# A two-layer trunk with a 32-expert mixture on one Trainium2 core: first quad gathered by single row blocks, slots compared with ranks in PSUM, layer one's means ahead of copies, four fillers ahead of mixer two

## What is computed

```python
def hierarchical_moe(x, wg, bg, we, be, w_gate, w_up, w_down):
    g_prob = softmax(xt @ wg + bg); g_top_p, g_idx = top_k(g_prob, 1)      # 1 of 4 groups
    e_top_l, e_idx = top_k(e_logits_of_that_group, 2)                      # 2 of its 8 experts
    gates = softmax(e_top_l) * g_top_p
    ...                                    # tokens are sorted by expert
    hb = silu(xb @ w_gate[e]) * (xb @ w_up[e])
    return hb @ w_down[e]                  # and summed with its gate into each token
```

## Time and profile before

| | |
|---|---|
| median of three runs | 1272.65 us (1272.19 to 1274.26) |
| the profiled execution, time | 1272.65 us |
| the profiled execution, span | 1270.9 us |
| TensorE matmuls busy | 1048.5 us, 83% of the span |
| VectorE busy | 477.2 us, 38% |
| ScalarE busy | 234.7 us, 18% |
| mean granted clock of TensorE | 0.903 of full speed |
| read from memory | 459.38 MB, 362 GB/s over the span |

### The profile page before, as it was taken

One profiled execution on the slowest core, in us unless ns is written; L12 is line 12 of the kernel. 1 busy time (PEld: TensorE's weight loads), 2 busy tenths in 40 slices (PEclk: granted clock), 3 DMA queues, 4 the chain that ended last, 5 costly groups with the idle time before them and its releaser, 6 DMA issues.

```text
span 1270.9 us, 22379 instructions
## 1 busy us (share of the span) xinstructions
PE 1048.5 (83%) x9528; PEld 712.1 (56%) x9528; DVE 477.2 (38%) x1227; ACT 234.7 (18%) x526; POOL 4.9 (0%) x27
## 2 busy tenths in 40 slices
PE   9999998966777575799999999998977676758685
PEld 7888755634433342448888888865544343424243
DVE  2342543342223222236665556464344222222232
ACT  2221121111111111113433334121111111111111
POOL 1000000000000000000000000000000000000000
PEclk9999998878788887899999999999898778878799
DMA  9888699999999999995666664999999999999996
GB/s 343 235 336 330 234 422 429 425 429 429 429 429 428 429 429 429 426 392 186 207 216 226 223 215 149 348 344 418 428 428 428 430 428 429 429 428 429 429 426 278
DMA packets 96049, 461.49 MB, mean 363 GB/s; under 512 B 17260, under 2 KB 60520, under 8 KB 70632
## 3 DMA queue, kind: packets, MB, share of 16 engines
q1 hardware_dynamic: 95616, 460.34, 90.1%
q10 hardware_dynamic: 360, 0.15, 0.0%
HBM read 459.38 MB, written 1.08 MB: 362 GB/s over the span
## 4 chain that ended last, share of the span: by engine, by line
PE 55%; DMA 40%; DVE 1%; issue 1%; SPq 1%; ACT 1%; POOL 0%; POOLq 0%; DVEq 0%; ACTq 0%
DMA front<-in_expert_w_up 33%; PE pa L1767 10%; PE pa L1487 10%; PE pb L1487 8%; DMA arena<-in_expert_w_down 5%; PE wa L1767 5%; PE acc L1518 4%; PE wb L1792 3%; PE acc L1625 2%; PE pb L1735 2%; PE acc L1802 1%; PE pb L1551 1%; PE pb L1726 1%; SPq L356 1%; PE pb L1836 1%
## 5 line engine op out<-in xcount | busy, mean ns | idle before, releaser
L1767 PE MATMUL pa<-front,arena 128*32 128x256 f32 x1792 | 137.0, 473 | 90.7 <-DMA front<-in_expert_w_up 90.7
L1767 PEld LDWEIGHTS pa<-front,arena 128*32 128x32 f32 x1792 | 66.7, 135 | 163.4 <-DMA front<-in_expert_w_up 103.2
L1245 DVE TENSOR_SCALAR lower<-lower 128x128 f32<-128x128 f32 x64 | 14.4, 225 | 382.6 <-ACT lower L583 382.6
L1767 PE MATMUL wa<-front,arena 128*32 128x256 f32 x1248 | 93.5, 463 | 64.5 <-DMA front<-in_expert_w_up 60.8
L1767 PEld LDWEIGHTS wa<-front,arena 128*32 128x32 f32 x1248 | 45.6, 132 | 112.8 <-DMA front<-in_expert_w_up 69.6
L583 ACT ACTIVATE arena<-wb 32x256 f32<-32x256 f32 (+2 forms) x236 | 88.9, 377 | 105.6 <-PE wb L1792 96.8
L1792 PE MATMUL wb<-w_dn,conv_raw 128*32 128x256 f32 x1472 | 87.8, 379 | 2.5 <-DMA w_dn<-in_expert_w_down 2.5
L1735 PE MATMUL pb<-arena,hs 128*128 128x128 f32 x448 | 67.6, 313 | 26.0 <-DVE arena L1161 11.3
L1487 PE MATMUL pa<-hnT,w_x 128*128 128x256 f32 x384 | 85.1, 380 | 0.0
L1735 PEld LDWEIGHTS pb<-arena,hs 128*128 128x128 f32 x448 | 61.7, 220 | 40.4 <-DVE arena L1177 18.6
L1487 PEld LDWEIGHTS pa<-hnT,w_x 128*128 128x128 f32 x384 | 72.5, 190 | 10.0 <-issue 0.3
(11 more groups left out here) (340 smaller groups left out, 1219.8 us busy)
## 6 DMA issues: line engine op xcount, KB each, us to landing
w_dn<-in_expert_w_down SPq DMA_DIRECT2D x46, 2048.0 KB, 26.0
front<-in_expert_w_gate SPq DMA_DIRECT2D x42, 2048.0 KB, 19.0
front<-in_expert_w_up SPq DMA_DIRECT2D x42, 2048.0 KB, 23.4
w_x<-in_expert_w_gate SPq DMA_DIRECT2D x15, 2048.0 KB, 30.3
w_x<-in_expert_w_up SPq DMA_DIRECT2D x15, 2048.0 KB, 34.6
arena<-in_expert_w_down SPq DMA_DIRECT2D x14, 2048.0 KB, 26.5
w_x<-in_odd_in_proj SPq DMA_DIRECT2D x16, 1024.0 KB, 5.4
front<-in_expert_w_up SPq DMA_DIRECT2D x8, 1024.0 KB, 9.3
```

What stands on the lines that cost most here:

```text
L1245: link(v.tensor_scalar(eg, eg, 1.0, None, ALU.add))
L1767: ins = mm(gu[32 * j:32 * j + 32, :, :], xb[:, k, c0:c0 + CAP], w[k][:, :, P * j:P * j + P], start=(k == 0), stop=(k == KC - 1))
```

## The change

Five edits:

1. Ranks in PSUM. The diagonal of `upper` is raised from 1 to 1001 (`raise_diagonal`, one DVE operation on 128x128), so a token that chose the expert has 1000 + rank, and one that did not has at most 256. `iota1` and `slot_id` start at 1001. Quad 0's `select_quad` reads the ranks in `wa` as they are, and `pos` is formed behind it. As mixer two uses `upper` as a plain mask, the diagonal is lowered behind expert 7 of mixture one and raised again ahead of mixture two.
2. `gather_first` and `gathered_first` take one row block instead of two: eight parts. DVE's operation becomes a `tensor_scalar` on 128x128. The eight stand at other places of DVE's list. `gu_half` is still raised after row blocks 1, 3 and 5, and PE waits for `pos` once more before it writes `wa`.
3. In the program's start each mean stands ahead of the copy.
4. `warm(4)` instead of `warm(7)`.
5. The counts of `gath_done` and `xs_done` follow (PARTS).

```diff
-PARTS = FIRST + 2 * (NE // QUAD - 1)
+PARTS = KC + 2 * (NE // QUAD - 1)
+FAR = 1000
...
+            def raise_diagonal(by):
+                link(v.scalar_tensor_tensor(upper[:, :], ident[:, :], float(by), upper[:, :], ALU.mult, ALU.add))
...
-                for t in range(TT):
-                    dve.wait_ge(S["x_t"], t + 1)
-                    v.tensor_copy(resT[:, 4 * t:4 * t + 4, 0:P], (pa, pb)[t][:, :].rearrange("p (k m) -> p k m", k=4)
-                                  ).then_inc(S["x_raw_dve"], 1)
+                mean(0)
+                turned_in(0)
+                mean(1)
+                turned_in(1)
...
+                select_quad(0, prk)
                 v.tensor_tensor(pos, prk, mask, ALU.mult).then_inc(S["mask_done"], 1)
                 dve.wait_ge(S["mask_done"], 2 * l + 2)
-                select_quad(0)
...
+                gathered_first(l, 0)
                 link(v.reciprocal(g1, s1))
                 link(v.tensor_tensor(g2, g1, e2, ALU.mult))
-                gathered_first(l, 0)
+                gathered_first(l, 1)
...
                 link(v.tensor_tensor(cols2, cols, over(other), ALU.mult))
                 link(v.tensor_reduce(out=at_other[:, 0:6], in_=cols2, axis=AX, op=ALU.add))
                 link(v.tensor_tensor(cols2, over(other), along(cols[:, :, WIDE:WIDE + 1]), ALU.mult))
+                gathered_first(l, 6)
                 link(v.tensor_tensor(cols, cols, over(keep), ALU.mult))
                 link(v.tensor_tensor(cols, cols, cols2, ALU.add))
                 link(v.tensor_tensor(cols2, over(here), along(at_other[:, 0:6].unsqueeze(2)), ALU.mult))
+                gathered_first(l, 7)
                 link(v.tensor_tensor(cols, cols, cols2, ALU.add))
...
-            def gathered_first(l, part):
-                dve.wait_ge(S["gath_done"], PARTS * l + part + 1)
-                k = slice(2 * part, 2 * part + 2)
-                v.tensor_tensor(xs[:, k, :], (XG, XG1)[part % 2][:, 0:2, :],
-                                nffn[:, l, k].unsqueeze(2).to_broadcast([P, 2, QUAD * CAP]), ALU.mult
+            def gathered_first(l, k):
+                dve.wait_ge(S["gath_done"], PARTS * l + k + 1)
+                v.tensor_scalar(xs[:, k, :], (XG, XG1)[k % 2][:, 0, :], nffn[:, l, k:k + 1], None, ALU.mult
                                 ).then_inc(S["xs_done"], 1)
...
                 gather_first(l, 0)
                 gather_first(l, 1)
-                for part in range(FIRST):
-                    if 0 < part < FIRST - 1:
-                        gather_first(l, part + 1)
-                    pe.wait_ge(S["xs_done"], PARTS * l + part + 1)
-                    ins = gate_up(xs, 0, early_cols(0), GU[0], ks=(2 * part, 2 * part + 1))
-                    if part < FIRST - 1:
+                pe.wait_ge(S["mask_done"], 2 * l + 2)
+                for k in range(KC):
+                    if 0 < k < KC - 1:
+                        gather_first(l, k + 1)
+                    pe.wait_ge(S["xs_done"], PARTS * l + k + 1)
+                    ins = gate_up(xs, 0, early_cols(0), GU[0], ks=(k,))
+                    if k % 2 and k < KC - 1:
                         ins.then_inc(S["gu_half"], 1)
...
-                    warm(7)
+                    warm(4)
```

More of the change, by code:

```diff
@@ L549, in _ @@
                            allow_small_or_imprecise_dtypes=True)
-            nc.gpsimd.iota(iota1[:, :], pattern=[[1, NE]], base=1, channel_multiplier=0,
+            nc.gpsimd.iota(iota1[:, :], pattern=[[1, NE]], base=FAR + 1, channel_multiplier=0,
                            allow_small_or_imprecise_dtypes=True)
@@ L556, in _ @@
             for q in range(4):
-                chain.link(nc.gpsimd.iota(slot_id[32 * q:32 * q + 32, :], pattern=[[0, 1]], base=1,
+                chain.link(nc.gpsimd.iota(slot_id[32 * q:32 * q + 32, :], pattern=[[0, 1]], base=FAR + 1,
                                           channel_multiplier=1, allow_small_or_imprecise_dtypes=True))
@@ L900, in _ @@
             link(v.tensor_scalar(descend[:, :], descend[:, :], 1.0 / 64, None, ALU.mult))
+            raise_diagonal(FAR)
             for m in range(2 * QUAD - 1):
@@ L918, in even_norm, with turned_in @@
                                     ).then_inc(S["mean_sq"], 1)
+                def turned_in(i):
+                    dve.wait_ge(S["x_t"], i + 1)
+                    v.tensor_copy(resT[:, 4 * i:4 * i + 4, 0:P], (pa, pb)[i][:, :].rearrange("p (k m) -> p k m", k=4)
+                                  ).then_inc(S["x_raw_dve"], 1)
+                mean(0)
+                turned_in(0)
+                mean(1)
+                turned_in(1)
                 dve.wait_ge(S["norm_cols"], 1)
@@ L1075, in route @@
                 link(ins)
+                gathered_first(l, 2)
                 link(v.tensor_tensor(gates, oh1, oh2, ALU.add))
-                gathered_first(l, 1)
             def swap_columns(l):
@@ L1090, in swap_columns @@
                 link(v.tensor_scalar(prefer, descend[:, :], 1.0, None, ALU.add))
+                gathered_first(l, 3)
                 link(v.scalar_tensor_tensor(prefer, iota[:, :], float(PRE), prefer, ALU.is_ge, ALU.mult))
                 link(v.scalar_tensor_tensor(prefer, cnt, float(CAP), prefer, ALU.is_gt, ALU.mult))
-                gathered_first(l, 2)
                 link(v.tensor_tensor(prefer, prefer, wide, ALU.max))
                 link(v.tensor_reduce(out=most, in_=prefer, axis=AX, op=ALU.max))
+                gathered_first(l, 4)
                 link(v.tensor_scalar(other, prefer, most, None, ALU.is_equal))
@@ L1099, in swap_columns @@
                 link(v.tensor_scalar(keep, keep, -1.0, 1.0, ALU.mult, ALU.add))
-                gathered_first(l, 3)
+                gathered_first(l, 5)
                 link(v.tensor_tensor(cols2, cols, over(other), ALU.mult))
@@ L1148, in select_rows, with select_quad @@
                                     [NE, 1, QUAD, CAP]), 1.0, None, ALU.mult).then_inc(S["prep_sel"], 1)
-            def select_quad(q):
+            def select_quad(q, ranks=pos):
                 v.tensor_tensor(quad_slots.rearrange("p t (e s) -> p t e s", e=QUAD),
                                 iota1[:, :].unsqueeze(1).unsqueeze(1).to_broadcast([P, TT, QUAD, CAP]),
-                                pos[:, :, ds(q * QUAD, QUAD)].unsqueeze(3).to_broadcast([P, TT, QUAD, CAP]),
+                                ranks[:, :, ds(q * QUAD, QUAD)].unsqueeze(3).to_broadcast([P, TT, QUAD, CAP]),
                                 ALU.is_equal).then_inc(S["quad_sel"], 1)
             def gathered(q, l, half):
-                dve.wait_ge(S["gath_done"], PARTS * l + FIRST + 2 * (q - 1) + half + 1)
+                dve.wait_ge(S["gath_done"], PARTS * l + KC + 2 * (q - 1) + half + 1)
                 k = slice(KC // 2 * half, KC // 2 * half + KC // 2)
@@ L1276, in moe @@
                         gathered(q + 1, l, 1)
+                    if l == 0 and e == LISTED - 1:
+                        raise_diagonal(-FAR)
                     if e == LISTED:
@@ L1731, in gather_quad @@
                     pe.wait_ge(S["g4_done"], NE * l + QUAD * q)
-                pe.wait_ge(S["xs_done"], PARTS * l + FIRST + 2 * (q - 1) + half)
+                pe.wait_ge(S["xs_done"], PARTS * l + KC + 2 * (q - 1) + half)
                 for k in range(KC // 2):
@@ L1748, in late_cols, with gather_first @@
                 return [(late3, late4)[e - 3][:, k // 4, :, k % 4, :] for k in range(KC)]
-            def gather_first(l, part):
-                if part == 0:
+            def gather_first(l, k):
+                if k == 0:
                     pe.wait_ge(S["quad_sel"], NE // QUAD * l + 1)
                     pe.wait_ge(S["hs_done"], 4 * l + 4)
[L1754 to L1759, removed]
+                if k > 1:
+                    pe.wait_ge(S["xs_done"], PARTS * l + k - 1)
+                for t in range(TT):
+                    ins = mm((XG, XG1)[k % 2][:, 0, :], hs[:, t, k, :], quad_slots[:, t, :],
+                             start=(t == 0), stop=(t == TT - 1))
                 ins.then_inc(S["gath_done"], 1)
@@ L1878, in middle_quad @@
                     gate_up(xs, CAP * j, gu_cols(s), GU[j % 2],
-                            2 * q + (PARTS * l + FIRST - 2) if j == 0 else None).then_inc(S["gu_done"], 1)
+                            2 * q + (PARTS * l + KC - 2) if j == 0 else None).then_inc(S["gu_done"], 1)
                     loads = uses(DSLOT, d, NE) * l + uses(DSLOT, d, before + 1) - LOOP[0]
@@ L1918, in moe @@
                         w = early_cols(e) if e == 1 else late_cols(e) if e in (3, 4) else gu_cols(s)
-                        gate_up(xs, CAP * j, w, GU[e % 2], PARTS * l + FIRST + 2 * (q - 1) if j == 0 else None,
+                        gate_up(xs, CAP * j, w, GU[e % 2], PARTS * l + KC + 2 * (q - 1) if j == 0 else None,
                                 half_sem=S["gu_half"] if e == 1 else None).then_inc(S["gu_done"], 1)
```

1 line of the change is left out of this document (added).

## The result

| | before | after |
|---|---|---|
| median of the runs | 1272.65 us | 1278.13 us |
| lowest and highest | 1271.5 to 1275.05 | 1276.0 to 1285.08 |
| ratio to before, 95% | | 1.0044 [1.0029, 1.0059] |
| the profiled execution, its span | 1272.65, 1270.9 | 1285.08, 1283.3 |
| its mean granted clock | 0.903 | 0.894 |

The kernel is 0.44% slower, 5.5 us, where no measurable change was forecast. The time of after lies above the whole range, 1269.6 to 1275.0. The profiled execution is the slowest of after's nine, so only single places are read from it, and what the change costs is taken from the ratio.

The account below looks back on a forecast made before the run. PE was taken to bound the mixers and DMA, at 431 GB/s, the mixtures. Gains of 0.5 for both mixtures, 0 for means and 0.6 for fillers sum to 1.1, from 1272.65 to 1271.5 us; range 1269.6 to 1275.0.

Parts of the forecast that it names:

- Selection from PSUM: Quad 0's selection in both layers: reading PSUM costs no more, so PE's gather starts 0.26 us earlier.
- First quarters: Each mixture's start: with single row blocks the first quarter of weights goes out 0.5 us earlier, the next two also.
- The last blocks: Last single row blocks of expert 0: DVE doesn't keep up, and PE is 1.2 us late from there on.
- The reload: Expert 6's weights: last load ahead lands 3.9 us behind the issue, 2.2 after; 0.25 more lost in each mixture.
- B: Rival at expert 6: queue dry before the new load moves, from 1.8 us of PE's lateness; 1275.5 us, chance 0.09.
- The queue that stands empty: Sign of being wrong: the DMA queue stands empty anywhere from 160 to 260 us.
- A stretch of lower clock ahead of the release: Within rival B, ahead of expert 6's release: 5.6 us at half speed, 2.8 us of work, makes PE 4.0 late.
- Means ahead of copies: Program's start: `hnT` could start a little earlier, but PE's first product waits for its weights; gain 0, bounds 0 and 0.1.
- Fillers: Ahead of mixer two: three fewer fillers free 0.69 us; 0.6 counted as gain, bounds 0 and 0.69.
- rival C: Fewer fillers cost clock: mixer two starts 2.8 us later, 1274.3 us, chance 0.06.
- Edits at nothing: `raise_diagonal`, near 0.29 us on a waiting DVE, and PE's new wait, met ahead of its first product, cost nothing.

Follow-up runs that it names:

- single blocks alone: The kernel before with only the single row blocks and their places in DVE's list added: 1278.73 us, 1.0040.
- pairs' kernel: The changed kernel with the gather put back to two row blocks at a time, the other edits kept: 1271.78 us, 0.9992.
- the turns: The kernel before with only PE's order inside parts 1 and 2 changed, turning between gather and gate/up eight times instead of four: 1276.71 us, 1.0023.
- the 16 products: The kernel before with 16 products of zeros between expert 1's gate and up and the positions, in both mixtures: 1279.62 us, 1.0044.
- early gates: Expert 3's rows and slot gates moved ahead of expert 2's down product: on before 1271.35 us, 0.9978; with the gather in pairs 1270.40 us, 0.9971.

## Why the prediction was wrong

**Selection from PSUM**: right. 0.42 us beside 0.43; the first gather product starts 1.19 behind the ranks where it was 1.46, so 0.27 earlier. The Trainium skill's longer fixed part for PSUM (VectorE: DVE Perf Modes, section on the TRN2 errata) doesn't show here.

**First quarters**: wrong in the size. A step that failed is "0.49 and 0.50 a block". It halved the pair's time as if a turn cost nothing, and a turn costs 0.19 and 0.14. The part on DVE lasts 0.35, not the 0.29 taken from a plain copy. So the first quarter goes out 847.74 - 843.35 = 4.39 behind the ranks where it was 840.40 - 835.86 = 4.54: 0.15 earlier, not 0.5. The next two come not 0.5 earlier but 0.18 and 0.5 later, at a rhythm of 2.42 rather than 2.1.

**The last blocks**: the mechanism was right, DVE's list is late and PE waits for it (0.52). But PE is 2.0 late, not 1.2. The 0.8 between lies in DVE's list: from L1078, the L1066 of before, to the last part are 853.85 - 844.60 = 9.25, where the working had 8.44. The seven parts ahead of it take 2.00 (from each start to that of the next operation 0.26 to 0.39), not 7 x 0.20 = 1.40, and waits for PE the other 0.2. PE's turns, 4 x 0.33 = 1.3 in all, add little here, since PE has to wait for DVE's last part all the same; by these rows it would still be 1.5 late without that wait. No run takes DVE's parts or the turns out of after alone.

**The reload**: this is the step that decided. The working took 3.9 us in hand from the landing of the last load ahead, and priced the loss at 0.25 a mixture. In the table the reload lands 3.6 later than 44.9 in after, and 2.6 later with the single blocks alone. The step that failed is to take a landing for the point where the queue falls empty: in after that load is issued at 868.56 and lands 19.5 later at 888.1, while nothing moves from 887 on and little from 886. The true margin was 3.9, less about 2 for that, less B's own 1.6 until a new load is at full rate: 0.3 at most, and none by the table. The queue that stands empty was also the sign by which the prediction would know itself wrong. B had the mechanism and the place, but wanted 1.8 us of lateness, and at 1.2 it was given a chance of 0.09. With 2.0 late and 0 to 0.3 in hand B is the forecast, even with the clock up: 1272.65 + 2 x (1.7 to 2.0), less 0.3 for the first quarters and 0.45 for the fillers, 1275.3 to 1275.9. The Trainium skill says it (DMA: Bandwidth & Descriptors, section on the anatomy of one DMA, there for the GpSimd path): of the fixed 2 us of a transfer most lies between its last byte and its semaphore. This trace, of SP's queue, agrees, with a landing at 888.1 behind the last bytes at 886 to 887.

**A stretch of lower clock ahead of the release**, B's price of 2.8 us: it happened, in both mixtures of after. It could account for the 2 to 3 us between that figure and the measured 1278.1 if it comes in most runs; see "still open".

**Means ahead of copies**: right. In the pairs' kernel PE's first product starts at 9.43, where before it was 9.36, with PE idle for 0.87 until the load is there:

```profile
9.43 1.10 PE L1566 MATMUL pb<-w_dn,hnT 128*128 128x256 f32 x4 [0.87 <-DMA w_dn<-in_even_w_in]
```

In after's profiled execution it starts at 10.97. The four transposes of one bank ahead of it take 1.06 there and 0.60 in the pairs' kernel, though the granted clock reads 1.00 in both; why is open. It doesn't go with this edit: such a start, at 10.47 to 10.97, stands in two of the seven profiled executions that have the edit and in three of the seven that haven't, and the others start at 9.26 to 9.53.

**Fillers**: near. In after L2017 starts 578.98 - 576.74 = 2.24 behind the last output product's group, before 2.69: 0.45 gained for 0.6, at a clock of 1.00. The prediction's rival C didn't happen. **Edits at nothing**: nothing speaks against it; the pairs' kernel holds them all and is no slower than before.

**Still open.** What makes the clock fall there. In 16 mixtures of the profiled executions PE has the pause of 1.08 ahead of the gather. In 5 of them the clock falls within 1.1 us of that gather's start and stays at 0.50 for 3.4 or 6.8 us, ahead of the reload: both of after, and one each of single blocks alone, of the turns and of the 16 products. In the 12 mixtures with early gates, where this pause is gone, it never does. It would also fit that early gates took 2.8 us from before and 2.7 from the pairs' kernel (0.9992 to 0.9971), where the landings of the table give 0.7 and nothing. And after's nine runs go with their mean granted clock: 1276.0 and 1276.8 us at 0.905, 1280.7 at 0.898, 1285.1 at 0.894; the fastest are near the 1275.3 to 1275.9 worked out above. The Trainium skill warns of idle gaps between bursts of matmuls (TensorE: Matmul & The Clock Gate, section on why this matters for your kernels); the gap here is 1.08 us. But that tie doesn't say which of the two brings the other, no run here holds the clock and changes nothing else, and only one execution of each kernel has a trace, so this is argued, not shown.

## What to carry to other kernels

Read slack at a queue from its bytes, not from landings: this queue was empty 1 to 2 us ahead of its last landing, and a new load needed 1.6 more. Don't price half of a group of products at half its time; look for a row of the smaller group or allow for the turn. Take a DVE operation's price from a row of its own kind: 0.35 here, where a copy's row has 0.29. And where PE is late ahead of a release, look for a pause just before it: moving expert 3's gates was worth more than the whole change had promised.

## What was not expected of the hardware

Turning between the gather (128 x 128 weights) and gate and up (128 x 32) costs PE 0.19 and 0.14 us; a wait that is already met costs nothing that can be seen. A DVE product of 128 columns from PSUM with a scalar per partition takes 0.35, where a plain copy of as many takes 0.29 and a product of two tensors of 256 columns takes 0.42. A load of 2 MB into an empty queue, with more close behind it, lands 7.9 to 8.8 us after its request; at the full queue's 431 GB/s 2 MB take 4.9.
